# Memory queries without their factor, rows turned later, other load and split order, matmuls on zeros first

## The reference

```
mkv = rms_norm(mem, mem_norm_g) @ mem_w_kv        # memory keys and values
a   = rms_norm(h, norm_g[0, 0])
q, k, v, g, mq = split(a @ ret_w_in)              # mq: memory queries
sc  = einsum(mq, mem_k) * MEM_HEAD_DIM ** -0.5    # 0.125
p   = softmax(sc); o = einsum(p, mem_v)
```

## Time and profile before

| | us |
|---|---|
| median of 3 runs | 2246.66 (2246.05 to 2247.91) |
| the profiled execution | 2245.32 |
| its span in the trace | 2243.5 |
| PE busy | 2208.0 |
| DVE busy | 1230.5 |
| POOL busy | 1116.7 |
| ACT busy | 881.5 |

### The profile page before, as it was taken

How to read it: one execution, slowest core, us unless ns; L and a number is a source line. 1 busy time by engine, 2 the same in 40 slices (tenths; PEclk the granted TensorE clock), 3 DMA queues, 4 the chain that set the end, 5 groups by cost and what they waited for, 6 DMA issues and landing times.

```text
span 2243.5 us, 31621 instructions
## 1 busy us (share of the span) xinstructions
PE 2208.0 (98%) x11614; PEld 1812.9 (81%) x11614; DVE 1230.5 (55%) x2064; ACT 881.5 (39%) x1770; POOL 1116.7 (50%) x889
## 2 busy tenths in 40 slices
PE   7999999999999999999999999999999999999998
PEld 6788888888888888888879877767878888888887
DVE  5744444647644444577773345465575444447767
ACT  6521111356232333344553345454732332334444
POOL 5133333468988888400334243325799878870001
PEclk9999999999999999999999999999999999999999
DMA  9021111342343333563354523243423433338334
GB/s 328 34 104 47 47 48 48 122 169 104 131 148 120 109 99 113 202 229 95 95 188 116 148 68 91 61 140 142 178 95 131 158 96 108 99 118 324 98 96 163
DMA packets 130823, 280.87 MB, mean 125 GB/s; under 512 B 31967, under 2 KB 46574, under 8 KB 128622
## 3 DMA queue, kind: packets, MB, share of 16 engines
q1 hardware_dynamic: 130670, 278.86, 37.9%
HBM read 208.03 MB, written 70.80 MB: 124 GB/s over the span
## 4 chain that ended last, share of the span: by engine, by line
PE 90%; POOL 3%; DVE 2%; ACT 1%; issue 1%; POOLq 0%; ACTq 0%; DVEq 0%
PE PS L2220 27%; PE PS L2222 27%; PE PS L2221 26%; PE PS L2493 2%; POOL OPS L950 2%; PE PS L2723 1%; PE PS L2705 1%; PE PS L2623 1%; PE PS L2526 1%; PE PS L2480 1%; PE PS L2610 0%; PE PS L2634 0%; PE PS L2238 0%; POOL TW L974 0%; PE PS L2636 0%
## 5 line engine op out<-in xcount | busy, mean ns | idle before, releaser
L2220 PE MATMUL PS<-AOP,OPS 128*128 128x512 f32 x1216 | 474.4, 390 | 2.4 <-POOL OPS L950 2.3
L2222 PE MATMUL PS<-AOP,OPS 128*128 128x512 f32 x1216 | 473.2, 389 | 0.0
L2221 PE MATMUL PS<-AOP,OPS 128*128 128x512 f32 x1216 | 473.2, 389 | 0.0
L890 POOL TENSOR_TENSOR wlo<-stage,whi 128x512 fp32r<-128x512 f32 (+1 forms) x176 | 228.7, 1325 | 326.0 <-ACT whi L1124 325.8
L950 POOL TENSOR_TENSOR OPS<-TW,OPS 128x512 fp32r<-128x512 f32 x176 | 265.5, 1523 | 77.1 <-ACT OPS L1218 77.1
L2220 PE MATMUL PS<-aT,whi 128*128 128x512 f32 (+1 forms) x672 | 272.0, 405 | 13.9 <-DVE aT L1632 10.1
L2220 PEld LDWEIGHTS PS<-AOP,OPS 128*128 128x128 f32 x1216 | 228.2, 188 | 52.6 <-POOL OPS L950 5.0
L2222 PEld LDWEIGHTS PS<-AOP,OPS 128*128 128x128 f32 x1216 | 228.2, 188 | 47.7
L2221 PEld LDWEIGHTS PS<-AOP,OPS 128*128 128x128 f32 x1216 | 228.3, 188 | 47.2
L2222 PE MATMUL PS<-aT,wlo 128*128 128x512 f32 (+1 forms) x672 | 260.2, 387 | 0.0
L2221 PE MATMUL PS<-aT,whi 128*128 128x512 f32 (+1 forms) x672 | 259.3, 386 | 0.0
(11 more groups left out here) (234 smaller groups left out, 4085.8 us busy)
## 6 DMA issues: line engine op xcount, KB each, us to landing
stage<-in_w SPq DMA_DIRECT2D x100, 512.0 KB, 3.9
hidden_scratch<-HT SPq DMA_DIRECT2D x154, 256.0 KB, 2.2
SRAW<-hidden_scratch SPq DMA_DIRECT2D x154, 256.0 KB, 2.7
stage<-in_wpack SPq DMA_DIRECT2D x76, 512.0 KB, 3.7
BW<-in_w SPq DMA_DIRECT2D x16, 1024.0 KB, 7.4
h_scratch<-Hb SPq DMA_DIRECT2D x24, 512.0 KB, 3.6
Hb<-h_scratch SPq DMA_DIRECT2D x24, 512.0 KB, 5.8
cat_scratch<-OC SPq DMA_DIRECT2D x14, 512.0 KB, 3.1
```

What stands on the lines that cost most here:

```text
L890: ins = pool.tensor_tensor(wlo[:, slot, cols], stage[:, slot, cols], whi[:, slot, cols].bitcast(F32), ALU.subtract)
L2220: pe.matmul(dst, stat[0], mov[0], start=start, stop=False, skip_group_check=onto)
L2221: pe.matmul(dst, stat[0], mov[1], start=False, stop=False, skip_group_check=onto)
L2222: return pe.matmul(dst, stat[1], mov[0], start=False, stop=stop, skip_group_check=onto)
```

## The change

`WARM` = 24 matmuls on the zeroed `bdK` are put on PE ahead of everything. Unit 1's high half is made between the memory's pieces 3 and 4. The last 512 tokens are loaded ahead of the rows to be squared, and split ahead of the squares, their first half of pieces ahead of unit 5's high part. The memory factors are turned in the middle of unit 5's first half, into bank 4; the memory values in the middle of its last half, into bank 7. DVE makes all low parts before the memory keys. The memory queries are copied by ACT as they are; `fac8` is each token tile's factor times 0.125, by partition (= token), used in `negmax` and as the exponential's scale. The tokens' factors are turned into rows behind attention step 0, and POOL's tables wait for the first `normalise`. Run 1 (layer 1) keeps the old form. The diff:

```diff
@@ -24,6 +24,8 @@
 RH = 6
 HP = 6
 ROWS, GW = 16, 64
+TOK_TILES = 8
+WARM = 24
 WR, WC = 8, 16
 HID = 2816
 KH = HID // P
@@ -145,6 +147,7 @@
     kprod = at("kprod", [P, 2, RH], F32, SM + 2432)
     halfsq = at("halfsq", [P, 12], F32, SM + 2560)
     Z = SM + 3 * KB
+    fac8 = at("fac8", [P, TOK_TILES], F32, SM + 2624)
     Y = at("Y", [P, TT, D], F32, Z)
     vfb = at("vfb", [P, 8, 2, P], F32, Z)
     qfb = at("qfb", [P, 2, SEQ], F32, Z)
@@ -265,7 +268,7 @@
 
 
         EV = {}
-        counts = {"a": RH, "d": 0}
+        counts = {"a": 0, "d": 0}
 
         def taken_by(n, who):
             counts[who] += 1
@@ -274,9 +277,10 @@
         for n in range(4):
             taken_by(n, "d")
         for n in range(2):
-            taken_by(U_RET + n, "d")
+            taken_by(U_RET + n, "a")
         for n in range(4 * RH):
             taken_by(U_RETH + n, "d")
+        counts["a"] += RH
         for n in range(2):
             taken_by(U_NA + n, "a")
         for n in range(2 * HP):
@@ -327,7 +331,7 @@
 
         def raw_come(t, k):
 
-            return (raw_ld[0], 32) if t == 0 else (raw_ld[1 + k // 4], 32) if t == 1 else (raw_ld[3], 64)
+            return (raw_ld[0], 32) if t == 0 else (raw_ld[1 + k // 4], 32) if t == 1 else (raw_ld[0], 64) if k < 4 else (raw_ld[3], 32)
 
         GAIN = [4, 0, 0, 1, 1, 2, 2, 3, 3]
         U_OUT = [U_OUT0, U_OUT1]
@@ -740,11 +744,13 @@
             load_raw(1, 2)
             load_raw(1, 3)
             load_units(5)
+            load_raw(2, 0)
+            load_raw(2, 1)
+            load_units(6)
+            load_raw(2, 2)
+            load_raw(2, 3)
             load_pre(0)
             load_pre(1)
-            load_units(6)
-            for part in range(4):
-                load_raw(2, part)
             for xi in range(2, 6):
                 load_pre(xi)
             load_units(7)
@@ -1038,13 +1044,13 @@
             pool.memset(bdK[:, :, :], 0.0).then_inc(zer, 1)
             pool.memset(kprod[:, :, :], 0.0).then_inc(zer, 1)
             pool.wait_ge(zer, 3)
-            los(5)
+            los(6)
             first_rms(0, 2)
             los(7)
             first_rms(2, 6)
             first_rms(6, 10)
             los(U_RETH + 2)
-            pool.wait_ge(*EV[U_RET])
+            pool.wait_ge(s_nrm, 1)
             pool.wait_ge(c_ld, 80)
             for table in (ropeC, ropeS):
                 pool.tensor_tensor(table[:, :], table[:, :], xrow[:, :], ALU.mult).then_inc(rope_on, 1)
@@ -1171,7 +1177,7 @@
 
                 if t == 0:
                     act.wait_ge(c_ids, 32)
-                if t == 2:
+                if t == 2 and 0 in part:
                     act.wait_ge(*USED[3])
                 for k in part:
                     act.wait_ge(*raw_come(t, k))
@@ -1393,7 +1399,8 @@
                         act.wait_ge(s_tr, r - 2)
                     for g in range(2):
                         ins = act.activation(SB[:, r % 3, MEM * g:MEM * g + MEM], memory_scores(r)[:, g, :],
-                                             ACT.Exp, bias=negmax[:, r % 4, g:g + 1], scale=0.125,
+                                             ACT.Exp, bias=negmax[:, r % 4, g:g + 1],
+                                             scale=fac8[:, r % 8:r % 8 + 1] if r < RUN_A0[1] else 0.125,
                                              accum_out=rowsum[:, r % 4, g:g + 1])
                     ins.then_inc(s_exp, 1)
                 else:
@@ -1444,19 +1451,26 @@
                        .then_inc(cat_hi, 1)
 
             his(1)
-            take_raw(0)
+            take_raw(0, range(4))
+            his(2)
+            take_raw(0, range(4, KD))
             his(3)
             take_raw(1, range(4))
             his(4)
             take_raw(1, range(4, KD))
             his(5)
+            take_raw(2, range(4))
+            his(6)
+            take_raw(2, range(4, KD))
             pre_x(0)
             pre_x(1)
-            his(6)
-            take_raw(2)
+            for xi in range(2, 6):
+                pre_x(xi)
             his(7)
-            for xi in range(2, 10):
+            for xi in range(6, 10):
                 pre_x(xi)
+            for n in range(2):
+                take(U_RET + n, MQ[:, n, :])
             his(U_RET + 4)
 
             def decays(t):
@@ -1902,7 +1916,12 @@
                 two = slice(r % 4, r % 4 + 2)
                 link(dve.tensor_reduce(maxraw[:, two, :], PS[:, 4:6, :].rearrange("p g (w c) -> p w g c", w=2),
                                        AX.X, ALU.max))
-                dve.tensor_scalar(negmax[:, two, :], maxraw[:, two, :], -0.125, None, ALU.mult).then_inc(s_add, 2)
+                if r < RUN_A0[1]:
+                    factors = fac8[:, r % 8:r % 8 + 2].rearrange("p (w c) -> p w c", c=1).to_broadcast([P, 2, 2])
+                    dve.scalar_tensor_tensor(out=negmax[:, two, :], in0=maxraw[:, two, :], scalar=-1.0, in1=factors,
+                                             op0=ALU.mult, op1=ALU.mult).then_inc(s_add, 2)
+                else:
+                    dve.tensor_scalar(negmax[:, two, :], maxraw[:, two, :], -0.125, None, ALU.mult).then_inc(s_add, 2)
 
             def peak(r, t, hp):
 
@@ -1987,12 +2006,11 @@
                     ins.then_inc(ev_dve, 1)
                     dve.wait_ge(*EV[n])
 
-            for t in range(2):
+            for t in range(3):
                 for k in range(KD):
                     raw_lo(t, k)
-            for k in range(4):
-                raw_lo(2, k)
-            keep_row(1, memrow[:, :], 3)
+            dve.wait_ge(t_done, 1)
+            link(dve.tensor_copy(memrow[:, :], PS[:, 4, MEM:2 * MEM]))
             dve.wait_ge(zer, 2)
 
             def memory_keys(n):
@@ -2010,13 +2028,11 @@
             memory_keys(1)
             memory_values(2)
             memory_values(3)
-            for k in range(4, KD):
-                raw_lo(2, k)
             dve.wait_ge(mvt, 1)
             dve.tensor_copy(memV[:, :, :].rearrange("p k (h f) -> p h k f", h=2),
-                            PS[:, 3, :].rearrange("p (h k f) -> p h k f", h=2, k=2)).then_inc(memv_rdy, 1)
-            for th in range(2):
-                keep_row(2 + th, xrow[:, HALF * th:HALF * th + HALF], 6 + th)
+                            PS[:, 7, :].rearrange("p (h k f) -> p h k f", h=2, k=2)).then_inc(memv_rdy, 1)
+            dve.wait_ge(pre_rs, 3)
+            link(dve.tensor_scalar(fac8[:, :], rstd[:, 2:2 + TOK_TILES], 0.125, None, ALU.mult))
 
             def take_scaled(n, dst, halves=range(2)):
 
@@ -2031,8 +2047,6 @@
 
                 dve.wait_ge(oc_st[h % 2], stored(h))
                 take_scaled(U_RETH + 4 * h + 3, OC[:, h % 2, :], halves)
-
-            take_scaled(U_RET, MQ[:, 0, :])
 
             def decays(t):
                 if t == 2:
@@ -2114,7 +2128,7 @@
             def gated_values(h):
                 g = h - 1
                 dve.wait_ge(aff, h)
-                dve.wait_ge(ev_act, h)
+                dve.wait_ge(ev_act, 2 + h)
                 c = h + 1
                 dst = output_place(c) if c in DIRECT else OC[:, c % 2, :]
                 for b in range(2):
@@ -2125,8 +2139,9 @@
 
             for t in range(steps(RUN_A0) + 1):
                 mem_step(RUN_A0, t)
-                if t == 1:
-                    take_scaled(U_RET + 1, MQ[:, 1, :])
+                if t == 0:
+                    for th in range(2):
+                        keep_row(2 + th, xrow[:, HALF * th:HALF * th + HALF], 6 + th)
                 decays(t)
                 for ago in range(4):
                     for u in units_done(t - ago, 4 * KD, steps(RUN_A0)):
@@ -2531,14 +2546,17 @@
 
             pe.wait_ge(c_ids, 32)
 
-            def turn_factors(n, first, tiles, bank):
+            def turn_factors(n, first, tiles, bank, at_c=0):
 
                 pe.wait_ge(pre_rs, n)
                 for i in range(tiles):
                     factors = rstd[:, first + i:first + i + 1].to_broadcast([P, P])
-                    ins = pe.transpose(PS[:, bank, i * P:(i + 1) * P], factors, ident[:, :])
+                    ins = pe.transpose(PS[:, bank, at_c + i * P:at_c + (i + 1) * P], factors, ident[:, :])
                 ins.then_inc(t_done, 1)
 
+            pe.wait_ge(zer, 2)
+            for _ in range(WARM):
+                pe.matmul(PS[:, 0, 0:P], bdK[:, 0, 0:P], bdK[:, 0, 0:P], start=True, stop=True)
             for n in range(4):
                 pe.wait_ge(w_lo, n + 1)
                 for k in range(KD):
@@ -2549,24 +2567,21 @@
                 ins.then_inc(w_used, 1)
 
             for k in range(KD):
-                if k == 4:
-                    turn_factors(1, 0, 2, 3)
                 project(U_RET, k, (0,), 1)
             for k in range(KD):
+                if k == 4:
+                    turn_factors(1, 0, 2, 4, MEM)
                 project(U_RET + 1, k, (0,))
-            pe.wait_ge(*EV[3])
-            for hp in range(2):
-                for kc in range(2):
-                    c = (2 * hp + kc) * P
```

(15 more changed lines are left out.)

## The result

| | median us (runs) | profiled execution, its span |
|---|---|---|
| before | 2246.66 (11) | 2245.32, 2243.5 |
| after | 2250.43 (11: 2249.09 to 2252.85) | 2251.26, 2249.5 |

The ratio is 1.0017 [1.0009, 1.0024]: 3.8 us slower. The interval leaves out 1, so this small loss is told from nothing, though it stays under the 0.2% that the prediction counted as no change. The forecast was 2246.4 and its range ended at 2249.0: the time lies 1.4 us outside.

What follows compares the result with a forecast made beforehand. TensorE, busy 98% of the span, bounds the kernel; only savings before 105 us count. +0.7 +1.3 +0.2 -1.6, taken as +0.4, and -0.7 give -0.3: 2245.0 profiled, 2246.4 median. Range 2242.0 to 2249.0.

Steps and rivals of the forecast that it cites:

- The split block: Start: POOL's weight halves hold up DVE's memory splits 4 to 7, last split at 17.7, unit 0 ends at 18.1.
- Rival A: Start: 256-column splits slip between POOL's, unit 0 ends at 14, 3 us gained, 2243.6; chance 0.20.
- The zeros: Kernel start: 24 matmuls from about 3.5 us, ending between 10.5 and 14.3, fully hidden by the split block.
- Unit 5's stall: Second query unit: PE waits for unit 5's low half, ready at 33.6 but wanted at 32.3, +1.3 us.
- The query unit: Behind units 0 to 3: the first query unit starts at 26.8 instead of 26.09, +0.7 us.
- the shift at scores 0: Attention's first scores: moved from 50.62 to 51.0, +0.4 us.
- The tables stand behind the first normalise and block the next negmax: Early attention: the block moves to the next DVE instruction, little gained; scores 4 at 63.85, -0.7 us.
- The decay constants were covered: Constants' load behind the memory stores: there at 57, used behind 61 us, 4 us of cover.
- units 1 to 3 back to back, 18.1 to 26.8: Behind unit 0: PE runs three units without the weight waits, 0.12 us per matmul, 8.65 us.
- Rival B: Unit 1: the clock falls back after the thin stretch from 12 to 17.7, 1.5 us lost, 2247.9; chance 0.16.
- the exponential gets its scale by row, so nothing: Attention's exponentials: the scale by row costs nothing, as operands scaled by row run at 0.41 for the same width.
- normalise to 56.1, tables 56.2 to 61.0: Early attention on DVE: first normalise, then tables, with the next negmax caught behind them to 61.15.

Runs made afterwards that it cites:

- y4: The changed kernel without its 24 matmuls on zeros in front; 2249.21 us, ratio 1.0010 to the kernel before.
- z2: The changed kernel with three more matmuls on zeros ahead of each of products 4 to 7 of unit 0; 2249.3 us, ratio 1.0011.
- x1b: The changed kernel with unit 1's split back behind all eight memory pieces, profiled again; one run of 2248.02 us.
- x2: The changed kernel with the constant 0.125 as the exponential's scale; 2247.16 us, ratio 1.0002.
- y2: The kernel before with only the attention part of the change, exponential's scale by row; 2246.64 us, ratio 0.9999.
- y3: The kernel before with only the attention part of the change and the constant 0.125 as the exponential's scale; 2244.96 us, ratio 0.9991.
- x3: The changed kernel with unit 5's high part ahead of the last 512 tokens' pieces; 2249.62 us, ratio 1.0006.
- x4: The kernel before with nothing but the 24 matmuls on zeros in front; 2248.14 us, ratio 1.0007.
- y5: The changed kernel with unit 1's split behind the memory pieces, no zeros and the constant exponential scale; 2246.09 us, ratio 0.9992.
- z1: The kernel before with the attention part, but the second query unit scaled by DVE and its exponentials at constant scale; 2245.70 us, ratio 0.9993.
- x1: The changed kernel with unit 1's split back behind all eight memory pieces; 2248.97 us over ten executions, ratio 1.0008.

## Why the prediction was wrong

**Right.** The split block came as forecast: DVE's last memory split ends at 17.9 where 17.7 was forecast, four pairs of 1.42; unit 0 ends at 18.4 (18.1). Rival A is out. (The Trainium skill's rule of the exclusive lock, "SBUF — State Buffer", named in the prediction, agrees for 256 columns and even for the negmax of four, 0.92 and 1.74 us beside POOL and 0.16 without.) The zeros start 0.8 us later than forecast (4.33) and end at 12.1, within 10.5 to 14.3; they are hidden in this kernel, since unit 0's last piece waits for DVE's split with them or without (y4). Unit 5's stall is 1.19 (1.3). The query unit starts at 28.56, less the fall 27.0 (26.8). Without the fall the shift at scores 0 is +0.46 (+0.4; z2 shows 51.14 for 51.0). The tables stand behind the first normalise and block the next negmax. The decay constants were covered: their load is issued at 51.55 and lands 4.6 us later, and ACT first reads them at 66.63, without a wait.

**Failed: the clock.** The step "units 1 to 3 back to back, 18.1 to 26.8" took 0.12 us for each matmul. Rival B, with a chance of 0.16 and priced at 1.5 us, held: fall at 19.15, 3.4 us at half clock, -1.49 when the empty stretch is filled (z2), absent where the split stands behind the memory pieces (x1b), present without zeros (y4). I argued against it that the clock read 1.00 throughout before; but between its first product and 130 us no stretch of before was as empty for as long as 14 to 18 us is after (1.61 us busy of 4; before's emptiest, 86.6 to 90.6, has 2.48). (The Trainium skill, "TensorE: Matmul & The Clock Gate", section "HAM oscillation — how this bites in real kernels", has such falls behind single waits for DMA that are several times longer than the 0.8 us here, so the prediction read it wider than it stands. The measurement decides: half clock came with no wait above 0.8 us.) I gave B a sixth of the chance on one observation, which did not cover the case. B alone, at 2247.9, would still have lain 2.5 us under the median.

**Failed: the term "the exponential gets its scale by row, so nothing".** Its price was read from SBUF operands that had the scale by row already (0.41), with no row without it to compare. It is +0.09 for each exponential, 0.36 for a pair of tiles. From scores 0 to scores 4 the forecast was 63.85 - 51.0 = 12.85, measured 13.58, so 0.73 was missed. One pair stands on the path there: 0.37 of the 0.73 is its price (3.06 us from negmax to scores 4, where x2 has 2.69 and the prediction took 2.7). The other 0.36 is a third miss, in the step "normalise to 56.1, tables 56.2 to 61.0": the first normalise ended 5.7 us behind scores 0 (58.32) where 5.1 was forecast, so the tables held the second negmax until 10.52 us behind scores 0, not 10.15; x2 has the same 10.51 with the constant scale. From scores 4 to 10 the scale by row costs 0.52 more, so that the forecast gain of 0.7 became a loss of 0.6. Both pairs of kernels show it (from scores 0 to 10, 0.91 after against x2, and 1.16 in y2 against y3, of which 0.26 is a second negmax that ends later). The Trainium skill ("ScalarE: Activation LUTs", section "What ACT_TABLE_LOAD costs") gives about 93 ns for each operand of an activation that is read by partition; the trace agrees with its 0.09.

**Sum.** Forecast -0.3; with the fall +1.55, the exponential +0.9 and the later block of the tables +0.4 it is +2.6, so 2249.3. The median is 1.1 above this.

**Open.** The falls at 94 and at 410 to 415. Behind 408 us PE waits 2.5 us for DVE in all these kernels; the profile of before has no fall there, those of x1b, x3, x4, y2 to y5, z1 and z2 have one, that of x2 none. Before's PE was even emptier there (0.02 us busy from 408 to 410 and 1.43 from 410 to 412, clock 1.00) than at 14 to 18 us after, so how empty PE is doesn't decide alone. What decides is not shown, nor whether the change makes it more frequent; the 1.1 us may lie there. The fall at 94 is in the profile of after alone, and x3 has the same waits at the same microseconds without it, so its cause is open too. By scores 4 x4's zeros cost 0.73, 0.3 more than at the query unit, not followed further.

## What to carry to other kernels

Before a split or a copy is moved ahead of others, look which engines block each other there, and what PE would be left with: three products every 1.4 us brought half clock for the full work behind them, which alone cost more (1.5 us) than the wait that the move took away (1.1), and the blocked splits cost 1.0 more. Price an instruction by a row with the same operands (bias and scale by row, from PSUM), not only the same width. Work taken off an engine that is not the bound gives back only the waits for it, and here the engine that took it up, ACT, was the one PE waited for.

## What the runs showed of the hardware

- Half clock came with a delay and outlasted the gaps: PE was emptiest from 14 to 18 us, the fall came at 19.15 when it had been full for 1.2 us, and it lasted 3.4 us of full work. In y4 it fell at 17.2, within the empty stretch, and in x3 it lasted 6.8 us.
- Filling the gaps with matmuls on zeros keeps the clock (z2), a burst of 7.8 us in front of the gap does not (after).
- Two executions of x1, one of them the profiled one, took 7873 and 5282 us for a kernel of 2249. In the profiled one the 24 zeros take 0.61 us each and the products of 256 columns stand 0.29 us apart, so it was slower than half clock (0.45 and 0.213). Its view gives a granted clock of 1.00 throughout, as before's does ahead of 13.5 us where the products stand 0.213 apart, so it doesn't tell the level. The two are left out of the comparison; nothing in the kernel explains them, since ten other executions and one profiled later took 2247 to 2250. The cause is open.
- A two-input DVE operation of 4 columns takes 0.16 us, and 1.74 beside POOL's 1024-column operation (after, 68.77 and 61.41 us).
- Two profiles with the same waits of PE at the same microseconds, ahead of 94 us, had different clocks behind them: 0.56 in after from 94 to 96, 1.00 in x3.
